# Two transformer blocks in one kernel: additions moved from TensorE to VectorE, raw-input start, reordered stage borders

## The reference, cut to what matters

```
# first block
x1 = rmsnorm(h) * norm_mix_g ; p = x1 @ w_in      # q, k, v, index, latent parts, two gates
o_a = attention over the 64 keys that an index score picks  (heads of 64, causal mask)
o_b = latent attention, heads of 96, causal mask
h += (sigmoid(g_a)*(o_a @ w_branch_a) + sigmoid(g_b)*(o_b @ w_branch_b)) @ w_out
h += (silu(gate)*val) @ w_down,  gate,val = causal_conv3(rmsnorm(h) @ w_up)   # 2816 wide
h = rmsnorm(h, norm_final_g)
# second block
h += hgrn2(rmsnorm(h))          # gated recurrence, 8 heads of 128
h += swiglu(rmsnorm(h))
h += attention(rmsnorm(h)): logits = q k^T / sqrt(128) + bias[head, distance], causal, softmax
h += swiglu(rmsnorm(h))
out = rmsnorm(h, final_norm_2)
```

## Time and profile before

| what | value |
|---|---|
| median of 3 runs | 1031.57 us (1031.29 to 1032.07) |
| the profiled execution's own time | 1032.62 us |
| its span | 1030.4 us |
| PE busy | 1002.3 us, 97% |
| DVE busy | 674.6 us, 65% |
| ACT busy | 545.6 us, 53% |
| POOL busy | 27.1 us, 3% |
| mean granted TensorE clock | 0.997 of full speed |

### The profile page before, as it was taken

The page is one execution under the profiler, slowest core; times in us unless marked ns, Lnnn a source line. Parts: engine busy times, 40 slices in busy tenths (PEclk is TensorE's granted clock), DMA queues, the critical chain, the costliest instruction groups (busy, mean ns, idle before and its releaser), DMA issues.

```text
span 1030.4 us, 15777 instructions
## 1 busy us (share of the span) xinstructions
PE 1002.3 (97%) x6433; PEld 860.0 (83%) x6433; DVE 674.6 (65%) x830; ACT 545.6 (53%) x706; POOL 27.1 (3%) x54
## 2 busy tenths in 40 slices
PE   7999999999999997999999999999999999999997
PEld 6888776898888886888789888888899888888885
DVE  5578755678787787968667655556644466555554
ACT  5776554456655665643546454454544546454452
POOL 2120000000000001000000000000000000000000
PEclk9999999999999999999999999999999999999999
DMA  9263333456655644754255655555654247565541
GB/s 298 71 213 116 130 123 127 145 178 204 204 171 195 198 149 148 241 179 154 84 184 184 204 197 176 197 197 174 223 163 143 103 137 243 193 202 174 194 163 41
DMA packets 121708, 175.78 MB, mean 171 GB/s; under 512 B 3040, under 2 KB 90419, under 8 KB 121651
## 3 DMA queue, kind: packets, MB, share of 16 engines
q1 hardware_dynamic: 118844, 168.82, 49.7%
q0 software_dynamic: 1264, 4.18, 1.4%
q10 hardware_dynamic: 1542, 1.96, 0.6%
HBM read 173.89 MB, written 1.06 MB: 170 GB/s over the span
## 4 chain that ended last, share of the span: by engine, by line
PE 87%; DVE 7%; ACT 3%; issue 1%; DMA 1%; POOL 0%; SPq 0%; POOLq 0%; DVEq 0%; ACTq 0%
PE ps L1726 26%; PE ps L1776 22%; PE ps L1747 11%; PE ps L1775 10%; PE ps L1763 4%; PE ps L1790 3%; DVE w_lo L1026 3%; PE ps L1798 2%; PE ps L1778 1%; ACT w_hi L506 1%; PE ps L1840 1%; PE ps L1993 1%; PE ps L2126 1%; PE ps L1979 1%; DMA raw<-in_w_in 1%
## 5 line engine op out<-in xcount | busy, mean ns | idle before, releaser
L1026 DVE TENSOR_TENSOR w_lo<-raw,w_hi 128x2048 fp32r<-128x2048 f32 (+3 forms) x162 | 364.6, 2253 | 134.6 <-ACT w_hi L506 134.3
L1776 PE MATMUL ps<-x_both,w_hi 128*128 128x512 f32 x992 | 342.8, 396 | 1.5 <-DVE w_lo L1026 1.5
L506 ACT ACTIVATE w_hi<-raw 128x2048 fp32r<-128x2048 f32 (+3 forms) x162 | 304.3, 1881 | 62.3 <-PE ps L1726 42.9
L1775 PE MATMUL ps<-x_both,w_lo 128*128 128x256 f32 x868 | 242.0, 279 | 0.0
L1776 PEld LDWEIGHTS ps<-x_both,w_hi 128*128 128x128 f32 x992 | 179.1, 188 | 36.2 <-issue 1.7
L1775 PEld LDWEIGHTS ps<-x_both,w_lo 128*128 128x128 f32 x868 | 163.6, 189 | 5.5
L734 ACT ACTIVATE work<-ps 128x512 f32<-128x512 f32 x66 | 39.3, 596 | 151.8 <-PE ps L1776 135.9
L1726 PE MATMUL ps<-w_hi,x_both 128*128 128x512 f32 (+2 forms) x352 | 111.0, 387 | 0.7 <-ACT work L662 0.5
L1747 PE MATMUL ps<-w_hi,x_both 128*128 128x512 f32 x288 | 96.2, 402 | 2.7 <-DVE x_both L1326 1.9
L1726 PE MATMUL ps<-w_hi,hid_hi 128*128 128x512 f32 x248 | 97.0, 391 | 0.6 <-issue 0.6
L1726 PE MATMUL ps<-w_hi,hid_lo 128*128 128x512 f32 x248 | 96.5, 389 | 0.0
(11 more groups left out here) (258 smaller groups left out, 1236.3 us busy)
## 6 DMA issues: line engine op xcount, KB each, us to landing
raw<-in_ffn_w SPq DMA_DIRECT2D x66, 1024.0 KB, 5.0
raw<-in_w_up SPq DMA_DIRECT2D x22, 1024.0 KB, 5.1
raw<-in_hgrn_w_in SPq DMA_DIRECT2D x16, 1024.0 KB, 5.5
raw<-in_w_in SPq DMA_DIRECT2D x12, 1024.0 KB, 6.5
raw<-in_moba_w_in SPq DMA_DIRECT2D x12, 1024.0 KB, 5.2
raw<-in_w_down SPq DMA_DIRECT2D x11, 1024.0 KB, 5.0
raw<-in_w_out SPq DMA_DIRECT2D x4, 1024.0 KB, 5.1
raw<-in_hgrn_w_out SPq DMA_DIRECT2D x4, 1024.0 KB, 5.7
```

Source lines behind the costliest of these rows:

```text
L506: act.activation(w_hi[:, n % RING, 0:kc * cols], raw[:, n % RING, 0:kc * cols], ACT.Copy).then_inc(s["hi_ready"], 1)
L1026: dve.tensor_tensor(w_lo[:, n % RING, sl], raw[:, n % RING, sl], f32(w_hi[:, n % RING, sl]), ALU.subtract).then_inc(s["lo_ready"], 1)
L1775: pe.matmul(out[:, 0, :], w_lo[:, n % RING, at], x_hi[:, k, :], start=False, stop=False)
L1776: ins = pe.matmul(out, w_hi[:, n % RING, at], x_both[:, k, :, :], start=(k == 0), stop=(k == DC - 1))
```

## The change

- The first projections use the raw rows of x; the inverse norm is applied where they are copied from PSUM. The first granule comes in two loads, and its high parts are multiplied first. The identity and the first gains are loaded by ACT's queue. The angle arithmetic moves behind `lo(3)` and the squares of the latent parts; copies of gains, taps and bias move behind `c_scaled`. POOL's inverse norm now waits for a DVE step behind `lo(2)`, and its three loads (L434 to L436) stand behind it.
- Masks of units 6 to 12 are added by DVE, out of PSUM into `prob`; maxima and exponentials read them there. DVE's `lo` of units 5, 7, 9, 11 is split in halves over two units.
- The last outputs of the first attention are split as they come, so that branch a waits tile by tile.
- The bias table is written to DRAM 128 times over (1.57 MB) and read back skewed, so that the reversing matrix goes; DVE adds the bias in `probm`.
- The first down product of the first feed-forward and the last one of feed-forwards 0 and 1 go high parts first; the adds of the first token tile wait per column.
- Before the recurrent mixer, `lo(nf)`, the normed h and the two clearings go to POOL; the gate bounds go into units 9 and 12. In the mixer `lo(nh + 8)` goes from level 5 to level 6.
- Before the second attention the first value products go all high parts first.

```diff
+MASKED_BY_DVE = range(6, 13)
-        bias_scratch = nc.dram_tensor("bias_scratch", (HEADS, BIAS_LEN), F32, kind="Internal").ap()
+        bias_scratch = nc.dram_tensor("bias_scratch", (P, HEADS, BIAS_LEN), F32, kind="Internal").ap()
@@ pool
-            pool.dma_start(const[:, K_ID:K_ID + P], a["const"][:, K_ID:K_ID + P]).then_inc(s["const_in"], 16)
...
                 power(var[:, 6 + t:7 + t], rstd[:, 6 + t:7 + t], s["var_ready"], 6 + 2 * t, s["rstd_ready"])
+                if t == 0:
+                    n = G["hf"]
+                    pool.wait_ge(s["row_ready"], step(3, 0, 1))
+                    pool.wait_ge(s["hi_ready"], n + 1)
+                    pool.wait_ge(s["lo_ready"], n)
+                    pool.tensor_tensor(w_lo[:, n % RING, :], raw[:, n % RING, :], f32(w_hi[:, n % RING, :]), ALU.subtract).then_inc(s["lo_ready"], 1)
...
+            for t in range(TT):
+                pool.wait_ge(s["rstd_ready"], 7 + t)
...
+                pool.tensor_tensor(h[:, t, :], scaled[:, t, :], rstd[:, 4 + t:5 + t].broadcast_to((P, D)), ALU.mult).then_inc(s["h_final"], 1)
+            pool.memset(near.rearrange("p a b -> p (a b)"), 0.0)
+            pool.memset(pairs.rearrange("p a b c -> p (a b c)"), 0.0).then_inc(s["pairs_zero"], 1)
@@ act
+            first_operand_hi(0, 2)
+            act.wait_ge(s["first_in"], 16)
+            act.activation(w_hi[:, 0, 0:first_cols], raw[:, 0, 0:first_cols], ACT.Copy).then_inc(s["first_hi"], 1)
+            first_operand_hi(2, 4)
+            act.wait_ge(raw_in[0], 16)
+            act.activation(w_hi[:, 0, first_cols:2 * first_cols], raw[:, 0, first_cols:2 * first_cols], ACT.Copy).then_inc(s["hi_ready"], 1)
+            first_operand_hi(4, 8)
+            hi_of(1, 2)
             for t in range(TT):
                 act.wait_ge(x_in[t], 16)
                 act.activation(xn[:, t, :], h[:, t, :], ACT.Square, accum_out=ssq[:, t:t + 1]).then_inc(s["ssq_ready"], 1)
...
+            act.dma_start(bias_scratch.rearrange("t h j -> h t j"), bias_row.unsqueeze(1).broadcast_to((HEADS, P, BIAS_LEN))).then_inc(s["bias_out"], 16)
...
-                return ps[:, 2 + u % 2, S * j:S * j + S], prob[:, u % 2, j, :]
+                return (prob[:, u % 2, j, :] if u in MASKED_BY_DVE else ps[:, 2 + u % 2, S * j:S * j + S]), prob[:, u % 2, j, :]
@@ dve
-            normalize(0)
-            lo(0)
-            first_operand_lo()
+            first_operand_lo(0, 4)
+            first_lo(0, s["first_hi"])
+            first_lo(1, s["hi_ready"]).then_inc(s["lo_ready"], 1)
+            first_operand_lo(4, 8)
             lo_of(1, 2)
+            for t in range(TT):
+                variance(0, t)
+            lo(3)
...
+                if u >= 16:
+                    j = (u - 16) // 2
+                    biased = probm[:, u % 2, :, 0:n]
...
+                    then(dve.tensor_tensor(biased, src, bias[:, 2 * j:2 * j + 2, S - n:S], ALU.add))
+                    src = biased
+                elif u in MASKED_BY_DVE:
+                    add = (add_b if u < 8 else add_a)[:, u % 2, :].unsqueeze(1).broadcast_to((P, 2, S))
...
+                    then(dve.tensor_tensor(prob[:, u % 2, :, :], src, f32(add), ALU.add))
+                    src = prob[:, u % 2, :, :]
...
+                elif u in (5, 7, 9, 11):
+                    lo_half(g0 + 2 + u // 2, 0)
                 elif u % 2 == 1:
                     lo(g0 + 2 + u // 2)
-                if u in (13, 15):
-                    gate_branch_b(u // 2 - 6)
+                elif u in (6, 8, 10, 12):
+                    lo_half(g0 + 1 + u // 2, 1)
...
+                if j == 0:
+                    dve.wait_ge(s["h_final"], 2)
...
-                if level < 6:
+                if level < 5:
                     lo(nh + 3 + level)
+                if level == 6:
+                    lo(nh + 8)
@@ pe
-            keep_busy(7, 7)
-            turn_xn()
+            keep_busy(7, 4)
+            turn_x(0)
...
+            first_product(0, 0)
+            first_product(1, 4)
...
-                pe.matmul(ps[:, 2 + u % 2, :], ident_r[:, :], add, start=True, stop=False)
+                if not by_dve:
+                    add = (add_b if u < 8 else add_a)[:, t, :].unsqueeze(1).broadcast_to((P, 2, S))
+                    pe.matmul(ps[:, 2 + u % 2, :], ident_r[:, :], add, start=True, stop=False)
...
-            pe.wait_ge(s["o_copied"], 16)
+            def out_ready(t, k):
+                pe.wait_ge(s["olo_ready"], 2 if k < 2 else 1 + 2 * t if k == 2 else 4 + t)
...
+                def last_down_high_first(p, n):
+                    at = 3 + PAIRS * f + p + 1
+                    pe.wait_ge(s["hhi_ready"], at)
+                    pe.wait_ge(s["hi_ready"], n + 1)
+                    for x, w in ((hid_hi, w_hi), (hid_lo, w_hi), (hid_hi, w_lo)):
+                        if x is hid_lo:
+                            pe.wait_ge(s["hlo_ready"], at)
+                        if w is w_lo:
+                            split_ready(n)
...
-                down_tile(10, n0 + 32, 0, signals=(3,))
+                last_down_high_first(10, n0 + 32)
...
-                    pe.matmul(dst, qm_T[:, head, P * t:P * t + P], km_T[:, head, 0:n], start=True, stop=False)
-                    ins = pe.matmul(dst, reverse, bias[:, head, S - n:S], start=False, stop=True)
+                    ins = pe.matmul(dst, qm_T[:, head, P * t:P * t + P], km_T[:, head, 0:n], start=True, stop=True)
```

More of the change, by code:

```diff
@@ L832, in square_both @@
                     square(2, t, c)
+                for c in range(2):
                     n = 2 * t + c
@@ L1327, in _ @@
+                if u == 15:
+                    gate_branch_b(1)
+            units(0, 16, fill_lo, lambda u: gate_branch_b(0) if u == 14 else None)
+            output_lo1(15)
             ba = G["branch_a"]
@@ L1497, in _ @@
                 operand_lo(3, 0, half)
[L1498 to L1499 removed]
+            add_scaled(1)
             both_variances(1)
@@ new lines, in _, with in_block, first_product @@
+            turn_x(0)
+            pe.wait_ge(s["mix_in"], 16)
+            pe.transpose(ps[:, 4, 0:8], vrow[0:8, 0, :], ident[0:8, 0:8]).then_inc(s["vrow_T"], 1)
+            turn_x(1)
+            keep_busy(7, 2)
+            def in_block(b, k):
+                token_product(2 * b + k, 4 * k, 4 + 2 * (b % 2), k == 0, k == 1)
+            def first_product(n, chunks):
+                _, _, _, kc, _, cols = granules[n]
+                for low in range(2):
+                    if low:
+                        split_ready(n)
+                    for k in range(kc):
+                        if not low:
+                            first_ready(chunks + k)
+                            if n == 0 and k == 0:
+                                pe.wait_ge(s["first_hi"], 1)
+                            if n == 1 or k == 2:
+                                pe.wait_ge(s["hi_ready"], n + 1)
+                        for t in range(TT):
+                            for x, w in (((x_hi, w_lo),) if low else ((x_hi, w_hi), (x_lo, w_hi))):
+                                ins = pe.matmul(ps[:, 4 + t, 0:cols], x[:, chunks + k, P * t:P * t + P], w[:, n % RING, cols * k:cols * k + cols],
+                                                start=(n == 0 and not low and k == 0 and x is x_hi), stop=(n == 1 and low == 1 and k == kc - 1))
+                ins.then_inc(s["products_done"], 1)
```

343 lines of the change are left out of this document (205 added, 138 removed).

## The result

The changed kernel takes 1021.53 us (median of 4 runs, 1021.23 to 1021.9), beside 1031.82 us (1031.29 to 1032.7) for the kernel before on the same chip: ratio 0.9898, 95% interval 0.9883 to 0.9914. It is faster, as forecast, but by 10.3 us instead of 21: the forecast of 1010.6 us is 10.9 us too low, and the time lies 3.5 us above the top of the range. The profiled execution took 1021.69 us, its span is 1019.8 us.

The account below looks back on a forecast made before the run. PE was taken as the bound, busy 1002.3 of 1030.4 us, so gains were instructions off PE and PE's waits. Eight terms summed to 21.0 us off 1032.62 us, 1011.6, or 1010.6 us as median; range 1006 to 1018 us.

Parts of the forecast that it names:

- the bias part: Second attention's bias: 16 PE products go; the 1.57 MB write, waited for only at 173 us, was costed at nothing.
- Start: First projections: raw rows and split weight loads let PE start near 9 us; 4.1 us less (2.5 to 5.0).
- its extreme form: Rival: slow bias write holds the DMA engines, weight loads wait; slower than before from 29 us of blocking; chance 0.02.
- The wait near 39 us: Start: `lo(5)` and the index rotation ready at 39.1 us, PE there at 38.3; 4.1 us of gain left.
- Masks: First attention, units 6 to 12: DVE adds the masks, 7 x 0.24 = 1.7 us less (0.8 to 2.3).
- End of first attention: Splitting outputs as they come removes PE's wait and the clock loss near 173 us: 3.7 us (2.0 to 3.8).
- First down product: First feed-forward: PE's wait for the low hidden part, 234.56 to 235.31 us, goes: 0.7 us (0.3 to 0.75).
- Into the mixer: Border into the recurrent mixer: high parts first and work moved to POOL shorten PE's waits: 4.4 us (2.0 to 5.5).
- the first rival: POOL and DVE block each other; the mixer border gives only 1.5 to 2.5 us: 1013 us; chance 0.17.
- Levels: Recurrent levels: `lo(nh + 8)` leaves the path from level 5's scaling to level 7's products: 0.55 us (0.3 to 0.6).
- Into the second attention: PE's waits near 724 and 730.68 us shrink, 0.95 us for the second tile's split stays: 0.75 us (0.2 to 1.2).
- Bias: Second attention: 16 bias products leave PE, DVE adds instead: 5.1 us less (4.5 to 5.2).

Follow-up runs that it names:

- the write moved: The changed kernel with the issue of the 1.57 MB bias write moved from 34 us to unit 4 of the first attention: 1014.09 us, ratio 0.9819.
- the run with early products: Late-write kernel (1014.1 us) with PE's filling products on the identity replaced by products from 1.1 us on a tile set by DVE: 1012.39 us, ratio 0.9809.
- the run with the weight ahead: Kernel with late write and early filling products (1012.4 us), the load of the first granule's first half issued ahead of the second tile's rows: 1014.01 us, ratio 0.9821.

## Why the prediction was wrong

The step that failed is one sentence of the bias part: the write "is only waited for at 173 us; I cost it at nothing". It asked who waits for the write, and not who shares the engines with it. In its place the runs showed a wait of 4.54 us and some 5 us at half the clock behind it, 7.1 us in all.

- **Start, forecast +4.1, measured -4.65.** The part that the edits of the start made was real: 2.45 us with the write moved. The write took 7.1 us of it back (85.25 against 78.15 us): 4.54 us of waiting, the rest at half clock. The prediction had the means to see it: it gave the loads behind the write "some 8 us of slack", and the three landed 10.7 to 14.4 us later than they do without it. It priced that mechanism only in its extreme form (29 us of blocking, slower than before) and gave it 0.02; a block of 11 to 14 us was worth two thirds of the miss. The slack itself was near what it said: `w_uq` was 10.7 us late and ACT waited 3.80 us for it, so 6.9 us were covered. The remaining 1.65 us of this term: the first product at 11.3 instead of 9.0 us. The turns stood behind 1.9 us of filling products and took 0.24 us each; with both mended the first product still came only at 10.21 us, for the weight's first half had landed at 9.05 instead of near 8 us. The wait near 39 us, for which the prediction took off 0.9 us, did not come: with the write late the lead is 2.49 us at the first turns and 2.45 us at unit 0. That is just below the prediction's lower bound of 2.5; of its reasons the lower clock is not shown by the clock's rows (1.00).
- **Masks, 1.7; measured 1.41.** Right, with 0.24 us a unit in most; DVE kept up.
- **End of first attention, 3.7; measured 3.24.** Right in mechanism: no wait and no clock loss at 173 us.
- **First down product, 0.7; measured 0.80.** Right.
- **Into the mixer, 4.4; measured 4.89.** Right in size, partly wrong in how: POOL and DVE blocked each other as the first rival said, for 0.91 us where I had counted 0.7, and POOL's subtraction took 4.61 us (estimate 5.2). That rival's rule, from the Trainium skill (SBUF — State Buffer, SBUF: two separate sides), fits the rows: operations with two SBUF inputs stretched, those with one in PSUM did not. Its cost did not outweigh what POOL took over: without POOL's work the first level's products come 0.91 us later. PE's wait for the second token tile is 0.84 us, not 2, and the granted clock stayed 1.00 from 396 to 412 us: the 1.7 us that the prediction left in its range for a fall did not come.
- **Levels, 0.55; measured -0.41.** The moved low part gave what was forecast. With the masks on PE, a version whose code in this stage is the same, the level of 64 products comes 4.08 us before the next one, 4.70 us in the kernel before, and the stage takes 46.62 us, 0.66 less than the 47.28 of before. What failed is the premise that PE's small products run on: in the changed kernel two rows of them break, at 466.50 and 491.64 us, and lose 0.65 and 0.42 us. PE's rows of the kernel before, the run with the masks on PE, and the changed kernel:

```profile
495.73 1.21 PE L2126 MATMUL ps<-work 128*32 128x32 f32 x64 [0.26 <-DVE work L1576]
```

```profile
484.25 1.21 PE L2275 MATMUL ps<-work 128*32 128x32 f32 x64 [0.25 <-DVE work L1657]
...
488.33 2.08 PE L2275 MATMUL ps<-work 128*64 128x64 f32 x32
```

```profile
466.50 0.27 PE L2274 MATMUL ps<-work 128*32 128x32 f32 x8 [0.45 <-issue]
...
491.64 0.69 PE L2274 MATMUL ps<-work 128*32 128x32 f32 x30 [0.18 <-issue]
```

  Nothing that the profile shows ends these breaks. In the fourteen versions with this code the stage takes 46.6 us (three of them, without a break) to 47.9 us. The cause is open.
- **Into the second attention, 0.75; measured 0.38**, at the low end of its range: 1.07 us of waiting stayed, where 0.95 had been forecast.
- **Bias, 5.1; measured 5.00.** Right.

The range was too narrow because the one unknown whose price no row gave stood in it with zero. A block of 12 us less the 8 us of slack, and 2.6 us of clock, would have added 6.6 us to the 1010.6 us; with the start at its lower bound (1.6 us) that is 1018.8 us, an estimate made after the fact, and an end of the range a few us above it would have held the measured time.

## What to carry to other kernels

A transfer that nobody waits for is not free: ask how many source partitions it reads, how its outermost dimension divides, and which loads are issued while it runs; then put it where the loads have slack. When an instruction waits late in its engine's order, moving it helps only if the load itself is on time. Where a stage is wholly PE's, instruction counts times distances of starts forecast to 0.3 us; what crosses queues needs a bound of its own.

## What the runs showed of the hardware

- A write of 1.57 MB from 8 SBUF partitions made three other loads 10.7 to 14.4 us late, with the DMA engines 61% busy at 117 GB/s. The same size from 128 partitions made them at most 1.5 us late, and copies from DRAM to DRAM with 128 copies or 8 heads outermost 0 to 5.2 us late.
- 127 against 128 copies as outermost dimension: 1050.5 against 1014.2 us.
- After PE had idled 4.54 us (5.16 us) its granted clock was 0.50 (the lower level, 1.2 GHz) for the next 5 us; it also fell after 1.87 us (twice, at one place) and 2.25 us. It stayed 1.00 (2.4 GHz) after 1.01 us, after 1.93 us, and after 2.43 us before the first product of the run with early products (1.00 from 9.5 to 13 us). So the length of the idling alone did not decide it here.
- At the very start the turns took 0.24 us each where PE had done plain products from 4.70 us on, and 0.14 us where it had done them from 1.07 us on; the rows' granted clock says 1.00 for both. In the run with the weight ahead, with the same early products, the first tile's 8 turns took 1.64 us, 0.2 us each: the speed was not the same in both.
- PE's rows of small products in the mixer broke in eleven of fourteen versions and lost up to 1.3 us a run, with nothing in the profile that ends the breaks.
